# The recurrent block's six projected tiles as three quads of seven products

## The chip, the cores and the metric

The kernel runs on one core of one Trainium2 chip. The metric is device time in microseconds of one execution, as the median of several runs. Engines are TensorE (PE), VectorE (DVE), ScalarE (ACT), GpSimd (POOL) and SyncE (SP), which issues all DMAs. Each has a queue of its own and runs it in order; they are tied together by semaphores alone. All data is 32-bit float.

## What is computed

A stack of layers over 528 positions of width 1024. The change touches the first mixer, a gated recurrence of width 1536, cut here to what matters:

```python
def recurrent_mixer(x, w_in, conv_w, conv_b, w_r, b_r, w_i, b_i, lam, w_out):
    gr = x @ w_in
    gate, rec = gr[..., :D_RNN], gr[..., D_RNN:]
    rec = causal_dwconv(rec, conv_w, conv_b)          # width 4
    h = rg_lru(rec, w_r, b_r, w_i, b_i, lam)
    return (jax.nn.gelu(gate) * h) @ w_out

def rg_lru(x, w_r, b_r, w_i, b_i, lam):
    r = sigmoid(block_diagonal(x, w_r) + b_r)
    i = sigmoid(block_diagonal(x, w_i) + b_i)
    log_a = -LRU_C * r * softplus(-lam)
    a = exp(log_a)
    u = sqrt(-expm1(2.0 * log_a)) * (i * x)
    h_t = a_t * h_{t-1} + u_t                          # a scan over positions
```

## The kernel before

Features lie on the 128 partitions, positions along the row. The 1536 features of the recurrence are 12 tiles of 128, done in four groups of three. A group uses 8 weight units of 512 KB (`units`), which SP brings in order into the four slots of `W` (`w_ring`); the rule for when a slot may be overwritten is `slot_left`.

One group before, on PE (`with pe.Fori(0, 4)`): three dense tiles for the convolved half, a fourth for one gate, each a full product of 8 contraction steps by two halves of 264 positions, 16 matmuls (L2126, in `gemm`). Then the two block-diagonal products of the group (L2294, 28 matmuls), which wait for the three convolutions (`lru_conv`) and read them (`rc`). Then two more gate tiles. Tiles go through four PSUM buffers of two banks; `tile_full` and `tile_free` count them. ACT copies each tile from PSUM to `xp`, does the first convolution tap (L2471), the gelus, the sigmoids, exponentials and roots. DVE does the other three taps (`lru_conv`, L2729 and L2731), the squares (L2738, L2739), then for each tile two multiplies and the scan (L2743 to L2745) and the last multiply into `A` (L2748). POOL has nothing to do in this stage. When the last group is done, `lru_out` begins, the output projection.

`lru_out` and all feed-forward layers use another scheme, in `quads` (L2191). Two output tiles by two halves of the positions, with the contraction cut in two halves, are a 2 x 2 by 2 x 2 matrix product of blocks, and that is done with seven block products in place of eight. Four sums of weight blocks are made first by POOL (L2823, L2826, L2828, L2831, function `weights`), four sums of the moving blocks by DVE (`moving`, L2549 to L2557), and the results are put together from PSUM by copies on ACT (L2360) and sums on DVE (for instance L2675). Products are numbered 1 to 7 and run as 1, 2, 6, 7, 4, 5, 3; products 1, 6, 7, 4 add up in one bank, from which ACT copies a state after each of them ("kept" 1 to 4); the others are added to a kept state by DVE, giving results "11", "22" and "12", while kept 4 is "21". Two quads, each with 14 products together, run side by side, so that while PE does a product of one, the copies and sums of the other are made.

## Time and profile before

| | |
|---|---|
| median of 3 runs | 3436.01 us (3434.14 to 3436.01) |
| the profiled execution | 3435.82 us |
| its span | 3434.1 us |
| PE busy | 3265.1 us, 95% |
| DVE, POOL, ACT busy | 1686.8, 1121.7, 1031.5 us |
| recurrent stage | about 6 to 219 us |

The page lists busy time by engine, the chain of work that ended last and the costliest groups of instructions. The timeline gives each engine's instructions in order of time, merged where neighbours are alike, with the idle time before them and its releaser in brackets. A matmul of 32-bit data leaves two records, so "x32" is 16 matmuls, and a product of a quad with four contraction steps is eight records. PE records overlap: the start of the next group is the better end of a group than start plus length.

### The profile page before, as it was taken

What the parts mean: (1) busy time and instruction counts of PE and PEld (TensorE: products, weight loads), DVE (VectorE), ACT (ScalarE), POOL (GpSimd) and SP (SyncE); (2) the same over time, 40 slices, a digit from 0 to 9 for tenths busy, and PEclk for the clock granted to TensorE, in tenths of its full rate; (3) what the DMA queues carried; (4) which work ended last, traced back from release to release, by engine and by line L of the source; (5) the groups of instructions that cost most, each with busy time, mean ns of one, the idle gap of its engine ahead of it and who ended that gap; (6) DMA issues with size and microseconds to landing.
All of it is one profiled execution on the core that took longest, in us unless ns stands there. A gap on an engine that the chain in (4) does not pass through costs nothing.

```text
span 3434.1 us, 51574 instructions
## 1 busy us (share of the span) xinstructions
PE 3265.1 (95%) x16950; PEld 2639.6 (77%) x16950; DVE 1686.8 (49%) x2837; ACT 1031.5 (30%) x2083; POOL 1121.7 (33%) x908
## 2 busy tenths in 40 slices
PE   9999999989998999998999999989999899799997
PEld 7787888867776788886546787868888588688886
DVE  3454546464445445644446545354553534355544
ACT  3433232122332323212316333123321334222311
POOL 0023344432221335441001333434444232353543
PEclk9999999999999999998999999989999899999999
DMA  3222222211111222221210211212222121122222
GB/s 119 79 86 92 79 92 80 92 68 51 54 50 38 74 83 82 80 92 56 68 55 19 62 55 55 80 55 92 79 92 82 66 68 63 50 74 91 85 92 74
DMA packets 68670, 249.36 MB, mean 73 GB/s; under 512 B 7568, under 2 KB 7568, under 8 KB 68544
## 3 DMA queue, kind: packets, MB, share of 16 engines
q1 hardware_dynamic: 68544, 247.72, 21.1%
q8 instruction: 75, 1.23, 0.1%
q14 instruction: 51, 0.42, 0.0%
HBM read 245.59 MB, written 2.10 MB: 72 GB/s over the span
## 4 chain that ended last, share of the span: by engine, by line
PE 88%; DVE 7%; issue 2%; ACT 2%; DMA 0%; DVEq 0%; POOL 0%; ACTq 0%; SPq 0%; POOLq 0%
PE psum L2191 54%; PE psum L2126 10%; PE psum L434 6%; PE psum L1745 3%; PE psum L1303 3%; PE psum L1330 1%; PE psum L1770 1%; PE psum L2294 1%; PE psum L466 1%; PE psum L1357 1%; PE psum L504 1%; DVE residual L2652 1%; PE psum L2245 1%; DVE stream L2650 1%; ACT scratch L1036 1%
## 5 line engine op out<-in xcount | busy, mean ns | idle before, releaser
L2191 PE MATMUL psum<-scratch 128*128 128x256 f32 (+1 forms) x3600 | 816.7, 383 | 12.3 <-ACT scratch L2360 6.4
L2191 PEld LDWEIGHTS psum<-scratch 128*128 128x128 f32 x3600 | 684.4, 190 | 120.2 <-ACT scratch L2360 8.9
L2823 POOL TENSOR_TENSOR scratch<-w_ring 128x512 f32<-128x512 f32 (+2 forms) x160 | 201.7, 1261 | 1374.1 <-DMA w_ring<-units 807.2
L2360 ACT ACTIVATE scratch<-psum 128x264 f32<-128x264 f32 (+1 forms) x480 | 185.0, 387 | 890.2 <-PE psum L2191 855.2
L2675 DVE TENSOR_TENSOR scratch<-scratch,psum 128x264 f32<-128x264 f32 (+1 forms) x264 | 108.3, 424 | 503.2 <-PE psum L2191 475.2
L2191 PE MATMUL psum<-scratch,w_ring 128*128 128x256 f32 (+1 forms) x1200 | 275.6, 382 | 0.0
L2191 PEld LDWEIGHTS psum<-scratch,w_ring 128*128 128x128 f32 x1200 | 227.9, 190 | 34.9
L2191 PE MATMUL psum<-acts,w_ring 128*128 128x264 f32 (+1 forms) x1088 | 247.1, 385 | 2.6 <-ACT scratch L2475 1.1
L2191 PEld LDWEIGHTS psum<-acts,w_ring 128*128 128x128 f32 x1088 | 207.7, 191 | 35.6 <-issue 2.5
L2423 ACT ACTIVATE scratch<-scratch,params 128x528 f32<-128x528 f32 (+1 forms) x176 | 144.4, 821 | 274.8 <-DVE scratch L2675 274.8
L2828 POOL TENSOR_TENSOR scratch<-w_ring 128x512 f32<-128x512 f32 (+2 forms) x160 | 226.5, 1416 | 0.0
L2831 POOL TENSOR_TENSOR scratch<-w_ring,scratch 128x512 f32<-128x512 f32 (+2 forms) x160 | 223.6, 1398 | 2.6 <-PE psum L2191 2.6
L2826 POOL TENSOR_TENSOR scratch<-scratch,w_ring 128x512 f32<-128x512 f32 (+2 forms) x160 | 219.5, 1372 | 12.6
L2682 DVE SCALAR_TENSOR_TENSOR scratch<-scratch,params 128x528 f32<-128x528 f32 (+1 forms) x176 | 201.6, 1145 | 25.5 <-DVE scratch L2680 8.9
L2680 DVE SCALAR_TENSOR_TENSOR scratch<-scratch,params 128x528 f32<-128x528 f32 (+1 forms) x176 | 203.9, 1158 | 0.0
L2126 PE MATMUL psum<-residual,w_ring 128*128 128x264 f32 (+1 forms) x800 | 181.9, 390 | 6.3 <-DMA residual<-x_t 6.3
L2126 PE MATMUL psum<-stream,w_ring 128*128 128x512 f32 (+1 forms) x400 | 178.6, 602 | 1.0 <-DVE stream L2637 1.0
L2126 PEld LDWEIGHTS psum<-residual,w_ring 128*128 128x128 f32 (+1 forms) x800 | 149.7, 188 | 37.9 <-issue 8.0
L2191 PE MATMUL psum<-residual,w_ring 128*128 128x264 f32 x704 | 165.3, 394 | 3.5 <-ACT residual L2407 3.5
L2191 PE MATMUL psum<-stream,w_ring 128*128 128x256 f32 x704 | 159.8, 386 | 1.9 <-DVE stream L2637 1.9
L2191 PEld LDWEIGHTS psum<-residual,w_ring 128*128 128x128 f32 x704 | 137.0, 195 | 28.3 <-issue 4.0
L2191 PEld LDWEIGHTS psum<-stream,w_ring 128*128 128x128 f32 x704 | 136.6, 194 | 21.7 <-issue 2.5
(454 smaller groups left out, 4732.9 us busy)
## 6 DMA issues: line engine op xcount, KB each, us to landing
w_ring<-units SPq DMA_DIRECT2D x463, 512.0 KB, 3.6
residual<-x_t SPq DMA_DIRECT2D x4, 528.0 KB, 7.0
out_t<-residual SPq DMA_DIRECT2D x4, 512.0 KB, 2.7
params<-cols SPq DMA_DIRECT2D x1, 568.5 KB, 9.1
gate_w_sb<-gate_w SPq DMA_DIRECT2D x1, 96.0 KB, 11.2
```

Source lines behind the costliest of these rows:

```text
L434: mm = nc.tensor.matmul(fx_bank(p), weights(k), moving(k), start=(p in (1, 2, 5) and k == 0), stop=(k == 3), skip_group_check=True)
L2126: mm = nc.tensor.matmul(PS[0:m1 - m0, bank + b, 0:n], W[:, s, q, m0:m1], rhs(k)[:, t:t + n], start=(k == 0), stop=(k == slots[-1][1] + slo ...
L2191: mm = nc.tensor.matmul(out, weights(k), moving(k), start=(p in (1, 2, 5) and k == 0), stop=(k == h - 1), skip_group_check=(p != 2))
L2360: nc.scalar.activation(kept(q, n, H), quad_bank(q, p, H), ACT.Copy).then_inc(q_copied, 1)
L2423: nc.scalar.activation(y[:, j, 0:T], xp[:, j, 0:T], ACT.Identity, bias=w(3), scale=w(0)).then_inc(shared("tap", name), 1)
L2675: v.tensor_tensor(xp[:, row, at:at + H], kept(q, keep, H), quad_bank(q, p, H), ALU.add).then_inc(q_added, 1)
L2680: c(v.scalar_tensor_tensor(out=y[:, j, 0:T], in0=xp[:, j, 1:1 + T], scalar=PAR[:, ds(w0 + 1, 1)], in1=y[:, j, 0:T], op0=ALU.mult, op1=ALU. ...
L2682: v.scalar_tensor_tensor(out=y[:, j, 0:T], in0=xp[:, j, 2:2 + T], scalar=PAR[:, ds(w0 + 2, 1)], in1=y[:, j, 0:T], op0=ALU.mult, op1=ALU.ad ...
L2823: g.tensor_tensor(s(1), row(1, 0), row(1, 1), ALU.add).then_inc(q_weight, 1)
L2826: g.tensor_tensor(s(2), s(1), row(0, 0), ALU.subtract).then_inc(q_weight, 1)
L2828: g.tensor_tensor(s(3), row(0, 0), row(1, 0), ALU.subtract).then_inc(q_weight, 1)
L2831: g.tensor_tensor(s(4), row(0, 1), s(2), ALU.subtract).then_inc(q_weight, 1)
```

## The change

The six projected tiles of a group (three for the convolution, three for the gates) become three quads m = 0, 1, 2, each making two tiles: quad 0 makes convolved tiles 0 and 1, quad 1 convolved tile 2 and gate 0, quad 2 gates 1 and 2. Quads 0 and 1 run side by side; quad 2 follows with its products 1, 2 and 6, the first block set, product 7, the second block set, and products 5, 4, 3. Units of the two block sets stand at the end of a group's eight. The loop over groups is written out on every engine. POOL makes twelve weight sums a group, DVE nine result sums, ACT twelve copies; the gelu now reads SBUF. The four moving sums of the input are made once, at the start, into `Z`. The start of SP's list is changed: the parameters come after the first four units.

```diff
+LQ_PRODUCTS = [(p, m) for p in (1, 2, 6, 7, 4, 5, 3) for m in (0, 1)] + [(p, 2) for p in (1, 2, 6, 7, 5, 4, 3)]
+LQ_WEIGHTS = [(n, m) for ns in ((1, 2), (3,), (4,)) for m in (0, 1) for n in ns] + [(n, 2) for n in (1, 2, 3, 4)]
+LRU_BANK = (0, 2, 6)
...
+                if name == "lru" and u < end:
+                    i, j = divmod(u, 8)
+                    if j >= 6:
+                        return [(tile_full, 6 * i + 3 * (j - 5))]
+                    return [(q_product, lq_done(i, j // 2, 4 if j % 2 else 2)), (q_weight, lq_weighed(i, j // 2, 3 if j % 2 else 4))]
...
+            for b in (2, 1, 3):
+                sp.dma_start(W[:, b, :, :], units[b]).then_inc(w_full[b], 16)
             sp.dma_start(PAR[:, :], cols).then_inc(loaded, 16)
-            for b in range(1, SLOTS):
-                sp.dma_start(W[:, b, :, :], units[b]).then_inc(w_full[b], 16)
...
+            for i in range(GROUPS):
+                for p, m in LQ_PRODUCTS[:14]:
+                    lru_quad(i, m, p)
+                for p in (1, 2, 6):
+                    lru_quad(i, 2, p)
+                pe.wait_ge(S("lru_conv"), 3 * i + 3)
+                pe.wait_ge(q_copied, lq_kept(i, 1, 4))
+                pe.wait_ge(q_added, lq_added(i, 1, "12"))
+                lru_blocks(i, 0)
+                lru_quad(i, 2, 7)
+                lru_blocks(i, 1)
+                for p in (5, 4, 3):
+                    lru_quad(i, 2, p)
...
+            for i in range(GROUPS):
+                lru_sum(i, 0, "11")
+                lru_sum(i, 1, "11")
+                if i:
+                    lru_scan(i - 1)
+                lru_sum(i, 0, "22")
+                lru_sum(i, 1, "22")
+                lru_conv(i, 1)
+                lru_sum(i, 0, "12")
+                lru_sum(i, 1, "12")
+                lru_conv(i, 0)
+                lru_sum(i, 2, "11")
+                lru_conv(i, 2)
+                if i == GROUPS - 1:
+                    dve.wait_ge(S("lru_act"), 9 + 1)
+                    for n in range(1, 5):
+                        moving(CHUNKS["lru_out"], n, 4, acts_of(0), HALF, T1)
+                lru_sum(i, 2, "22")
+                lru_squares(i)
+                lru_sum(i, 2, "12")
+            lru_scan(GROUPS - 1)
...
+            for i in range(GROUPS):
+                for n, m in LQ_WEIGHTS:
+                    lru_weights(i, n, m)
+            pool.wait_ge(q_product, lq_done(GROUPS - 1, 2, 3))
             down("lru_out")
```

In `lru_quad`, product 6 waits for weight sum 2 and kept state 1, product 7 for weight sum 3 and kept 2, product 4 for kept 3, product 5 for weight sum 1 and result "11", product 3 for weight sum 4 and result "22". `lru_sum` waits for its product and kept state. ACT's list in a group is: kept 1 of quads 0 and 1, the last group's roots, kept 2, gelus of the last group between kept 3 of quads 0 and 1, kept 4 and the taps, kept 1 and 2 of quad 2, sigmoids around its kept 3, exponentials and tanhs with its kept 4.

PE, the end of a group's first part and the first block set. Before (the fourth dense tile, then the wait for `lru_conv`):

```order
L2114 REGISTER_ALU [waits w_full3]
L2126 MATMUL psum<-residual,w_ring 128x264 [waits tile_free]
L2126 MATMUL psum<-residual,w_ring 128x264 x15
L2286 ISA
L2109 REGISTER_ALU [waits lru_conv]
L2114 REGISTER_ALU [waits w_full0]
L2294 MATMUL psum<-scratch,w_ring 128x264 [waits tile_free]
```

And now, from product 3 of quad 1 to the second block set (L2356 is a product, L2368 the blocks):

```order
L2356 MATMUL psum<-residual,scratch 128x264 [waits quad_added,quad_weight]
L2356 MATMUL psum<-residual,scratch 128x264 x3
L2356 MATMUL psum<-residual,w_ring 128x264 [waits w_full0,quad_copied]
L2356 MATMUL psum<-residual,w_ring 128x264 x3
L2356 MATMUL psum<-residual,w_ring 128x264 [waits w_full0,quad_added]
...
L2356 MATMUL psum<-stream,scratch 128x264 [waits quad_copied,quad_moving,quad_weight]
...
L2368 MATMUL psum<-scratch,w_ring 128x264 [waits w_full2,quad_added,tile_free,quad_copied,lru_conv]
...
L2368 MATMUL psum<-scratch,w_ring 64x264 x4
L2368 MATMUL psum<-scratch,w_ring 32x264 x4
L2356 MATMUL psum<-stream,scratch 128x264 [waits quad_copied,quad_moving,quad_weight]
...
L2368 MATMUL psum<-scratch,w_ring 128x264 [waits tile_free,w_full3]
```

The dense tile of 16 matmuls ahead of the wait for `lru_conv` has become three products of four, and a fourth stands between the two block sets.

DVE, around the squares and the scan. Before, in one row after the convolutions (L2738 and L2739 squares, L2743 to L2745 multiplies and scan):

```order
L2738 TENSOR_TENSOR scratch<-scratch 128x528 [waits lru_at]
...
L2739 SCALAR_TENSOR_TENSOR scratch<-scratch 128x528 [waits dve_chain]
...
L2743 TENSOR_TENSOR scratch<-scratch 128x528 [waits lru_sqrt]
...
L2744 TENSOR_TENSOR scratch<-scratch 128x528 [waits dve_chain]
...
L2745 SCALAR_TENSOR_TENSOR scratch<-scratch 128x528 [waits dve_chain]
...
L2747 ISA [waits dve_chain]
L2748 ISA [waits tile_free]
```

And now, from the last sum of group 0 on (L2866 is a result sum, L2888 to L2890 the scan of the last group, L2893 the last multiply, L2872 a convolution step):

```order
L2866 TENSOR_TENSOR scratch<-scratch,psum 128x264 [waits quad_copied,quad_product]
L2866 TENSOR_TENSOR scratch<-scratch,psum 128x264 [waits lru_conv,quad_copied,quad_product] x2
L2888 TENSOR_TENSOR scratch<-scratch 128x528 [waits tile_free,lru_sqrt]
L2889 TENSOR_TENSOR scratch<-scratch 128x528 [waits dve_chain]
L2890 SCALAR_TENSOR_TENSOR scratch<-scratch 128x528 [waits dve_chain]
...
L2893 TENSOR_TENSOR acts<-scratch 128x528 [waits lru_gelu,dve_chain]
...
L2866 TENSOR_TENSOR scratch<-scratch,psum 128x264 [waits lru_conv,quad_copied,quad_product]
L2866 TENSOR_TENSOR scratch<-scratch,psum 128x264 [waits lru_conv,lru_act,quad_copied,quad_product]
L2872 SCALAR_TENSOR_TENSOR scratch<-scratch,params 128x528 [waits lru_tap]
```

The scan and the multiplies of a group have moved behind the first two result sums of the next, and stand ahead of the two that follow.

## Rows read from the trace of the kernel before

**Rows 1.** The page: busy time (1), chain by engine (4).
```profile
PE 3265.1 (95%) x16950; PEld 2639.6 (77%) x16950; DVE 1686.8 (49%) x2837; ACT 1031.5 (30%) x2083; POOL 1121.7 (33%) x908
...
PE 88%; DVE 7%; issue 2%; ACT 2%; DMA 0%; DVEq 0%; POOL 0%; ACTq 0%; SPq 0%; POOLq 0%
```

**Rows 2.** Timeline of PE: start, length, record count; idle before in brackets.
```profile
99.62 42.99 PE L2126 MATMUL psum<-residual,w_ring 128*128 128x264 f32 x192
142.45 9.87 PE L2294 MATMUL psum<-scratch,w_ring 128*128 128x264 f32 x56
152.24 42.99 PE L2126 MATMUL psum<-residual,w_ring 128*128 128x264 f32 x192
```

**Rows 3.** Waits of PE, 0 to 240 us: total, times, longest.
```profile
PE psum L2191 <- ACT scratch L2475: 1.1, 1, 1.1
```

**Rows 4.** Windows: busy us by engine, PEclk, DMA share, GB/s.
```profile
100.00:150.00 50.00, 50.00 (x232) 41.28 (x230) 21.13 (x27) 23.55 (x31) 0.00 (x0) 1.00 0.24 78
```

**Rows 5.** Timeline of PE in the quads of lru_out.
```profile
245.92 7.28 PE L2191 MATMUL psum<-acts,w_ring 128*128 128x264 f32 x32
253.04 7.28 PE L2191 MATMUL psum<-acts,scratch 128*128 128x264 f32 x32
```

**Rows 6.** Tile w_ring, 353.8 to 355 us: DMA issues, time to landing.
```profile
L2090 SPq DMA_DIRECT2D w_ring<-units x2: 328/355/382, 353.6 to 354.0; - x2
...
DMA to landing us min/median/max: 3.5/4.0/4.4
```

**Rows 7.** Timeline of DVE and ACT, 57 to 74 us, POOL idle.
```profile
59.79 0.71 DVE L2743 TENSOR_TENSOR scratch<-scratch 128x528 f32<-128x528 f32 x1
...
62.57 0.71 DVE L2743 TENSOR_TENSOR scratch<-scratch 128x528 f32<-128x528 f32 x1
...
65.56 1.95 DVE L2748 TENSOR_TENSOR acts<-scratch 128x528 f32 x3 [0.25 <-DVE scratch L2745]
...
69.69 0.83 ACT L2471 ACTIVATE scratch<-scratch,params 128x528 f32<-128x528 f32 x1 [0.18 <-ACT scratch L2468]
...
72.52 0.77 DVE L2731 SCALAR_TENSOR_TENSOR scratch<-scratch,params 128x528 f32<-128x528 f32 x1
```

**Rows 8.** Timeline of DVE and POOL, 215 to 241 us, both busy.
```profile
217.06 1.66 DVE L2744 TENSOR_TENSOR scratch<-scratch 128x528 f32<-128x528 f32 x1
...
218.75 2.21 DVE L2745 TENSOR_TENSOR_SCAN scratch<-scratch 128x528 f32<-128x528 f32 x1
...
226.55 4.98 DVE L2748 TENSOR_TENSOR acts<-scratch 128x528 f32<-128x528 f32 x3
...
240.64 1.27 POOL L2823 TENSOR_TENSOR scratch<-w_ring 128x512 f32<-128x512 f32 x1 [7.98 <-PE psum L2191]
```

**Rows 9.** Lines L2675 (a DVE sum reading PSUM) and L2360: ns min/median/max, mean.
```profile
L2675 DVE TENSOR_TENSOR scratch<-scratch,psum x264: 411/423/431, 320.0 to 3277.6; 128x264 f32<-128x264 f32 x66, 128x256 f32<-128x256 f32 x66
...
L2360 ACT ACTIVATE scratch<-psum 128x264 f32<-128x264 f32 (+1 forms) x480 | 185.0, 387 | 890.2 <-PE psum L2191 855.2
```

**Rows 10.** Waits of DVE, 0 to 240 us.
```profile
DVE small L2708 <- DMA params<-cols: 12.3, 1, 12.3
```

**Rows 11.** Tile w_ring, first units: issue times and landing.
```profile
L2085 SPq DMA_DIRECT2D w_ring<-units x3: 432/451/870, 3.7 to 4.7; - x3
...
DMA to landing us min/median/max: 9.8/11.0/11.8
```

**Rows 12.** Timeline of PE, first group.
```profile
8.38 28.99 PE L2126 MATMUL psum<-residual,w_ring 128*128 128x264 f32 x124 [0.33 <-DMA residual<-x_t]
```

**Rows 13.** Idle PE and its clock after: timeline of PE, windows.
```profile
792.35 0.45 PE L488 MATMUL psum<-identity,scratch 128*128 128x128 f32 x1 [2.82 <-DVE scratch L667]
...
2945.87 7.13 PE L2191 MATMUL psum<-scratch 128*128 128x256 f32 x24 [4.98 <-POOL scratch L2826]
...
792.00:794.00 2.00, 1.65 (x5) 1.32 (x6) 1.01 (x5) 1.97 (x3) 2.00 (x3) 0.59 0.00 0
2946.00:2948.00 2.00, 2.00 (x6) 1.58 (x7) 0.00 (x0) 0.00 (x0) 2.00 (x2) 0.54 0.18 72
```

More of the change, by code:

```diff
@@ new lines, in lru_blocks, with piece @@
+            def lru_blocks(i, g):
+                s = unit(0, i, 8, 6 + g)
+                at = 3 * g
+                def piece(o, k, b, t, n, first=False):
+                    (r0, r1), (c0, c1) = LRU_CROSSED.get((o, k), ((0, P), (0, P)))
+                    return nc.tensor.matmul(PS[c0:c1, LRU_BANK[o] + b, 0:n], W[r0:r1, s, LRU_PIECES.index((o, k)), c0:c1],
+                                            rc[r0:r1, k, t:t + n], start=first, stop=not first, skip_group_check=True)
+                for o in range(3):
+                    pe.wait_ge(tile_free, 6 * i + (at + o + 1 + BUFS - 3))
+                    for b, t, n in parts(T1):
+                        piece(o, o, b, t, n, True)
+                for pair in LRU_PAIRS:
+                    for b, t, n in parts(T1):
+                        for o, k in pair:
+                            mm = piece(o, k, b, t, n)
+                            if b == 1 and (o, k) == (0, 1):
+                                mm.then_inc(tile_full, 1)
+                            if b == 1 and (o, k) == (2, 1):
+                                mm.then_inc(tile_full, 2)
@@ L2371, in down @@
                 for c in range(len(KS[name])):
+                    if name == "lru_out" and c == 0:
+                        body(0, b, (2, 3))
+                        body(1, b)
+                        continue
                     if name == "mix_out" and c == 0:
@@ L2493, in _ @@
+            lru_roots(GROUPS - 1)
+            copies(0, BODIES["lru_out"], T1, (1,))
+            for j in range(3):
+                lru_gelu(GROUPS - 1, j)
             project("lru_out", T1)
@@ L2546, in moving @@
                 if n == 1:
+                    if chunk == CHUNKS["lru"]:
+                        for q in range(4):
+                            dve.wait_ge(x_loaded[q], 16)
                     if chunk >= 2:
@@ L2911, in _layout @@
             put(a_in, RNN + (3 * g + j) * P)
-        put(a_in, 3 * g * P)
+        for j in range(3):
+            put(a_in, (3 * g + j) * P)
         for w in (f["a_w_r"][0], f["a_w_i"][0]):
@@ L2919, in _layout @@
             at[0] += 1
-        for j in (1, 2):
-            put(a_in, (3 * g + j) * P)
     at_phase("lru_out")
```

284 lines of the change are left out of this document (183 added, 101 removed).

## The prediction

> **What bounds the kernel now.** The page first: TensorE (PE) is busy for 95% of the span, and the chain that ended last is PE's work for 88% [rows 1]. So a stage is worth what PE spends in it. The timeline of PE in the recurrent stage comes next [rows 2]: each trip is one unbroken run of 192 records at L2126 and one of 56 at L2294 (every matmul leaves two records, and a product of four matmuls eight). From 99.62 to 142.45 us is 42.83 us for the 192, to 152.24 another 9.79 us for the 56: 52.62 us a group, no gap. Once the first input is there, PE waits for another engine once up to 240 us, for 1.1 us [rows 3]. VectorE (DVE) works 21 us in each 50 of this stage and GpSimd (POOL) not at all [rows 4]. The stage is bound by PE alone; the others have slack that the change spends.
>
> **What it removes.** A quad does 7 products of 4 matmuls for the 32 matmuls of two projected tiles. A group falls from 96 matmuls to 84. The existing quads show the pace: 32 records, 4 products, from 245.92 to 253.04 us, 7.12 us, or 1.78 us a product [rows 5]. 21 products are 37.4 us; with the blocks' 9.79 us, 47.2 us a group. Against 52.62 that is 5.45 us a group, **21.8 us in four groups**. The wait of 1.1 us for a gelu at the head of the output projection [rows 3] goes as well. All the rest of the change is waits, so I walked through one group, queue by queue; numbers that follow another engine's step include its wake-up, 0.2 to 0.3 us. E is the end of the second block set; a product is 1.78.
>
> **Weights, each boundary between groups.** Unit 9 may be fetched only after product 4 of quad 2, at E+3.56, and unit 10 stands behind it on SP's queue. PE has the product 3 and the next product 1, 3.56 us, before it reads unit 10. A row shows such a pair: issued 353.56 and about 0.47 later, landing after 3.5 and 4.4 us [rows 6], so the second is there 4.9 us after the first was issued. With 0.2 us to wake SP and 0.1 to wake PE: 5.2 - 3.6 = **1.6 us**, four times (the head of lru_out has it too). Bounds: 0.9 (landings 0.6 shorter) to 2.0.
>
> **DVE's queue, the scan.** The scan of the last group now stands between two quad sums. It starts when sum "11" of quad 1 is done: E + 5.34 (products 5, 4, 3) + 1.6 + 4 products + 0.3 + 0.43 = E+14.8. Alone its nine instructions take 3 x 2.78 us (59.79 to 62.57), the three multiplies 2.1 with their wake [rows 7]: done at E+25.2, and sum "22" of quad 0, due at E+26.8, is on time. But POOL now forms twelve weight sums a group. What this does is in the rows where POOL and DVE first meet [rows 8]: DVE instructions with both inputs in SBUF go from 0.71 us (at 59.79, [rows 7]) to 1.66, 0.95 us more for each POOL instruction beside them, and the scan from 1.26 to 2.21; three multiplies take 4.98 instead of 1.95 us. The sums that read PSUM stay at 0.42 us [rows 9]. POOL's eight sums for quads 0 and 1 run from E+7.5 (landing of unit 9) to about E+20.7, the four for quad 2 from E+26.9. The scan meets three to four of the first, the multiplies two of the others: 5.2 us. DVE reaches sum "22" at E+30.4, and product 3 of quad 0 starts at E+31.0 in place of E+28.3: **2.7 us**. Bounds: 0 (without the meetings) and 4.
>
> **DVE's queue, the convolution.** Before, the blocks waited for three convolutions under the gate tile of 7.2 us; now the cover is products 1, 2, 6 of quad 2, 5.34 us, after product 3 of quad 1. In that time DVE finishes conv 1, does sums "12" of quads 0 and 1, conv 0, sum "11" of quad 2 and conv 2. A tap is 0.83 us and ends at 70.52, the third instruction of its convolution at 73.29: 2.6 us and 0.17 to wake [rows 7]. With a POOL instruction beside conv 1, conv 2 ends 8.4 us after that product 3, PE asks at 5.34 + 0.4 (product 6 waits for a copy behind the taps): **2.8 + 0.4 us**, each group. Without POOL it is 2.1.
>
> These rows have DVE lose 0.95 us beside a POOL instruction that alone takes 1.27 [rows 8]. The Trainium skill ("SBUF — State Buffer", Who interferes with whom) has the loser of the shared port blocked for the other's whole instruction. By that, six meetings a group cost 0.3 us more each; the sum goes by the rows, and the rest is rival E.
>
> **The start.** The parameters move behind three weight units on SP. They landed at 12.3 us, when their first user on DVE started [rows 10]; unit 2 takes that place and lands at about 12.1, while product 1 of quad 0 is done at 9.3: 2.8. Then units 1 and 3 at about 13.7 and 15.1 (the three landed 9.8 to 11.8 us after issues at 3.7 to 4.7, [rows 11]), each with two POOL sums before product 6: 0.7 and 1.1 more, and the blocks' 2.8: **7.5 us** in group 0, where before lost 1.2 (124 records from 8.38 us to the first block set at 37.20, 28.8 us where 27.7 would do [rows 12]).
>
> **Head of lru_out.** 1.6 for weights; POOL starts only after the last product and makes four sums for quad 0 before two for quad 1: 1.6; DVE brings the scan, four operand sums and a full backlog, so that product 3 waits 4.0. **7.2 us**, where before had 1.1 and about 0.5 [rows 3, 5].
>
> **Hidden.** ScalarE gets 12 copies of 0.387 us [rows 9] for three of 0.61, about 2.8 us a group, beside a similar set of table loads; it is ahead of PE at each copy by my walk except at the 0.4 above. Writing out the loop removes register work on queues that had slack. SP and DMA volume are unchanged.
>
> **The sum.** -21.8 + 7.5 + 3 x (1.6 + 2.7 + 0.4 + 2.8 = 7.5) + 7.2 - (1.2 + 1.1 + 0.5 saved) = **+12.6 us**. The profiled execution took 3435.8 (a span of 3434.1 and 1.7 around it), the median run 3436.0; forecast **3448.6 us**.
>
> **Rivals.** (B) *The clock follows the stalls.* After PE idled 4.98 us for a POOL sum, up to 2945.87 us, the granted clock was 0.54, where 0.50 is 1.2 GHz and 1.00 is 2.4, and 24 records took 7.13 us, where at the pace of [rows 5] 5.3 and a record's tail of 0.16 would do: 1.6 us lost. After a wait of 2.82 us, up to 792.35, it was 0.59 [rows 13]; there sparse small matmuls stood before it, here a dense stretch would. My stalls of 2.7, 2.8 and 4.0 us lie about there. 1.0 to 1.6 us for each of some seven such stalls, partly swallowed by the next wait: +4 to +10, 3456 us. The Trainium skill ("TensorE: Matmul & The Clock Gate", The HAM clock gate) has the array at 1.2 GHz when it has been idle and at 2.4 when busy, which speaks for B; these rows agree. (C) *DVE keeps up.* It decides at product 3 of quad 0: if the scan and multiplies meet POOL for 2.7 us less than I count, that stall is gone in three groups (-8.1), the convolutions' falls by 0.3 in four (-1.2) and that of lru_out by 2: 3437 us. For it speaks that POOL's start hangs on landings that spread by 0.9 us [rows 6], and that the overlap is worked out, not seen; against it, that every SBUF instruction of DVE beside POOL in [rows 8] pays. (D) *They do not meet at all*, POOL's sums falling into DVE's idle time: what stays is weights 4 x 1.6, convolutions 4 x 2.1 and 3.5 at the start, 18.3 us against the 24.6 saved: -6.3, 3429.5 us, on the other side. The place is the same queue; it decides where fewer than about one in five of the meetings happens. Against it: POOL needs 15 to 20 us of a group's 47 (twelve of 1.27 to 1.7) and DVE 27, in one order for both. (E) *A meeting costs the whole POOL instruction*, 1.27 us: 6 x 0.32 x 3 groups, +5.8, 3454 us; a backlog carried from group to group would end there or above, to 3460.
>
> **Chances.** Forecast 0.44, B 0.16, C 0.24, D 0.10, E 0.06. The forecast's own range, from the bounds on landings and on the scan's stall, is 3441 to 3453. The range of 3430 to 3459 leaves out half of D and the upper parts of B and E. 0.2% is 6.9 us, about what a measurement here can tell from no change: faster than 3429.1 has 0.09 (most of D's low half and of C's tail), slower than 3442.9 0.62 (B, E and the forecast less its low edge), the same 0.29.
>
> **What would show it.** Products 1.78 us apart and groups 54.7 us apart; PE waiting for a DVE sum before product 3 of quad 0, for a DVE convolution before each block set, and for a DMA of w_ring at the second product of each group; DVE's SBUF instructions at 1.7 us beside POOL. The profile that proves me wrong has groups under 50 us apart and PE without waits of over 1 us, or multiplies at 0.65 us right before the sums.

## The result, and the profile after

| | before | the change |
|---|---|---|
| median | 3434.14 us (3430.58 to 3436.01, 7 runs) | 3445.65 us (3444.51 to 3453.97, 7 runs) |
| profiled execution, its span | 3435.82, 3434.1 us | 3451.29, 3449.6 us |
| PE busy | 3265.1 us | 3257.4 us |

The ratio is 1.0037, with an interval of 1.0027 to 1.0048: slower by 0.37%. The forecast was 3448.6 us, 12.6 above before; the medians are 11.5 apart. The profiled execution of the change is 5.6 us slower than its median, so what its trace shows, the granted clock above all, is one case and not the average. On the page PE has less work, and its part of the chain has gone from 88% to 84%, where [rows 1] stood before:

```profile
PE 3257.4 (94%) x16854; PEld 2625.3 (76%) x16854; DVE 1735.6 (50%) x2877; ACT 1028.3 (30%) x2111; POOL 1196.6 (35%) x956
...
PE 84%; DVE 9%; issue 3%; ACT 3%; DMA 1%; POOL 0%; DVEq 0%; SPq 0%; ACTq 0%; POOLq 0%
```

What PE waited for between 0 and 290 us (total, times, longest), where [rows 3] had one wait of 1.1 us for another engine:

```profile
PE psum L2368 <- DVE scratch L2874: 7.7, 4, 1.9
PE psum L2356 <- DMA w_ring<-units: 6.0, 4, 1.7
PE psum L2356 <- DMA residual<-x_t: 5.8, 1, 5.8
PE psum L2230 <- DVE stream L2726: 4.6, 1, 4.6
PE psum L2230 <- POOL scratch L2982: 1.8, 1, 1.8
PE psum L2356 <- DVE scratch L2866: 1.6, 2, 0.8
PE psum L2230 <- DMA w_ring<-units: 1.5, 1, 1.5
```

L2356 is a product of the recurrent quads, L2368 a block set, L2230 a product of `lru_out`; L2874 ends a convolution, L2866 is a result sum. The third group in PE's timeline, where [rows 2] had one unbroken run:

```profile
107.57 2.05 PE L2356 MATMUL psum<-stream,scratch 128*128 128x264 f32 x8
109.46 1.94 PE L2356 MATMUL psum<-stream,w_ring 128*128 128x264 f32 x8
...
113.02 1.94 PE L2356 MATMUL psum<-residual,w_ring 128*128 128x264 f32 x8
116.33 5.58 PE L2356 MATMUL psum<-residual,w_ring 128*128 128x264 f32 x24 [1.37 <-DMA w_ring<-units]
...
144.22 2.02 PE L2356 MATMUL psum<-stream,scratch 128*128 128x264 f32 x8 [0.96 <-ACT scratch L2553]
148.18 6.67 PE L2368 MATMUL psum<-scratch,w_ring 128*128 128x264 f32 x28 [1.94 <-DVE scratch L2874]
154.78 2.05 PE L2356 MATMUL psum<-stream,scratch 128*128 128x264 f32 x8
156.66 4.88 PE L2368 MATMUL psum<-scratch,w_ring 128*128 128x264 f32 x28
161.47 2.05 PE L2356 MATMUL psum<-stream,scratch 128*128 128x264 f32 x8
```

Three things are to be read here. Products are 1.78 us apart where nothing waits, as forecast. The second block set ends at 107.57 and 161.47: this group lasted 53.90 us (the four ends are 55.33, 107.57, 161.47 and 215.46, so 52.24, 53.90 and 53.99). And a wait costs 0.16 us more than its bracket: from 113.02 to 116.33 are 3.31 us for one product and a wait of 1.37, since the last record's tail of 0.16 is in the open. The first block set of this group took 6.67 us where the second took 4.88. The windows say why (columns: stretch, sum, PE, PEld, DVE, ACT, POOL busy, PEclk, DMA share, GB/s):

```profile
95.00:98.00 3.00, 2.04 (x9) 1.78 (x10) 0.87 (x2) 0.00 (x0) 0.00 (x0) 1.00 0.03 14
148.20:153.20 5.00, 5.00 (x16) 3.68 (x18) 0.00 (x0) 0.00 (x0) 0.00 (x0) 0.66 0.00 0
202.30:207.30 5.00, 5.00 (x18) 3.40 (x20) 4.62 (x4) 0.00 (x0) 0.00 (x0) 0.66 0.01 3
```

After one and the same wait of 1.94 us the granted clock stayed 1.00 in the second group and was 0.66 over the block set in the third and the fourth. The head of `lru_out` has three waits, and the third leaves a clock of 0.66 (251 to 256 us) too, 5.51 us for 16 records that take 3.72 elsewhere:

```profile
224.39 5.58 PE L2230 MATMUL psum<-acts,w_ring 128*128 128x264 f32 x24 [1.54 <-DMA w_ring<-units]
...
233.59 5.60 PE L2230 MATMUL psum<-acts,scratch 128*128 128x264 f32 x24 [1.84 <-POOL scratch L2982]
...
250.87 5.51 PE L2230 MATMUL psum<-acts,scratch 128*128 128x264 f32 x16 [4.56 <-DVE stream L2726]
```

DVE and POOL in the second group, from the start of the scan (L2888 to L2890) over the three multiplies (L2893) to sum "22" (L2866) and the first convolution (L2872):

```profile
70.09 0.70 DVE L2888 TENSOR_TENSOR scratch<-scratch 128x528 f32<-128x528 f32 x1
70.83 1.66 DVE L2889 TENSOR_TENSOR scratch<-scratch 128x528 f32<-128x528 f32 x1
72.53 2.20 DVE L2890 TENSOR_TENSOR_SCAN scratch<-scratch 128x528 f32<-128x528 f32 x1
74.77 1.60 DVE L2888 TENSOR_TENSOR scratch<-scratch 128x528 f32<-128x528 f32 x1
...
81.21 3.04 DVE L2893 TENSOR_TENSOR acts<-scratch 128x528 f32<-128x528 f32 x3
84.17 0.76 DVE L2866 TENSOR_TENSOR scratch<-scratch,psum 128x264 f32<-128x264 f32 x2
...
82.42 1.27 POOL L3000 TENSOR_TENSOR scratch<-w_ring 128x512 f32<-128x512 f32 x1 [6.62 <-DMA w_ring<-units]
```

Three instructions of the scan pay for a POOL instruction beside them, 0.9 us each, as in [rows 8]. Of the multiplies only one does (3.04 us for three, about 1.1 above their time alone), since POOL's next sums start at 82.42, when two of them are through. In the third group none does, in the fourth one, and PE waits before product 3 of quad 0 in the second and the fourth group alone (0.78 and 0.77 us):

```profile
133.42 1.95 DVE L2893 TENSOR_TENSOR acts<-scratch 128x528 f32<-128x528 f32 x3
...
187.49 3.02 DVE L2893 TENSOR_TENSOR acts<-scratch 128x528 f32<-128x528 f32 x3
```

The scan here doesn't wait for the roots, which ACT ends at 69.60 us, but for its place behind sum "11" of quad 1 (69.75 us).

### The profile page after: what moved, and what is told of

Read it like the earlier page. It is cut to its first block, busy times and chain, and to the rows that moved or that the text cites. A ratio compares the mean times of both kernels' runs of the same rounds, so it can differ in the third digit from the quotient of the medians.

```text
span 3449.6 us, 51443 instructions
## 1 busy us (share of the span) xinstructions
PE 3257.4 (94%) x16854; PEld 2625.3 (76%) x16854; DVE 1735.6 (50%) x2877; ACT 1028.3 (30%) x2111; POOL 1196.6 (35%) x956
## 4 chain that ended last, share of the span: by engine, by line
PE 84%; DVE 9%; issue 3%; ACT 3%; DMA 1%; POOL 0%; DVEq 0%; SPq 0%; ACTq 0%; POOLq 0%
PE psum L2230 53%; PE psum L473 6%; PE psum L2165 5%; PE psum L1784 3%; PE psum L1342 3%; PE psum L2356 2%; PE psum L1369 1%; PE psum L2368 1%; PE psum L1809 1%; PE psum L505 1%; PE psum L1396 1%; DMA w_ring<-units 1%; PE psum L543 1%; DVE scratch L2872 1%; DVE residual L2784 1%
## 5 line engine op out<-in xcount | busy, mean ns | idle before, releaser
L2230 PE MATMUL psum<-scratch 128*128 128x256 f32 (+1 forms) x3600 | 816.7, 383 | 12.2 <-ACT scratch L2444 6.4
L2230 PEld LDWEIGHTS psum<-scratch 128*128 128x128 f32 x3600 | 684.4, 190 | 120.1 <-ACT scratch L2444 8.8
L2230 PE MATMUL psum<-scratch,w_ring 128*128 128x256 f32 (+1 forms) x1200 | 275.6, 382 | 0.0
L2230 PEld LDWEIGHTS psum<-scratch,w_ring 128*128 128x128 f32 x1200 | 227.9, 190 | 34.9
L2230 PE MATMUL psum<-acts,w_ring 128*128 128x264 f32 (+1 forms) x1088 | 248.0, 385 | 3.4 <-DMA w_ring<-units 1.9
L2230 PEld LDWEIGHTS psum<-acts,w_ring 128*128 128x128 f32 x1088 | 207.8, 192 | 36.9 <-issue 3.7
L2982 POOL TENSOR_TENSOR scratch<-scratch,w_ring 128x512 f32<-128x512 f32 (+2 forms) x160 | 220.1, 1376 | 12.6
L2230 PE MATMUL psum<-residual,w_ring 128*128 128x264 f32 x704 | 164.7, 393 | 3.5 <-ACT residual L2495 3.5
L2230 PE MATMUL psum<-stream,w_ring 128*128 128x256 f32 x704 | 160.0, 387 | 1.9 <-DVE stream L2769 1.9
L2230 PE MATMUL psum<-acts,scratch 128*128 128x264 f32 (+1 forms) x624 | 149.5, 392 | 10.1 <-DVE stream L2726 7.5
L2230 PEld LDWEIGHTS psum<-residual,w_ring 128*128 128x128 f32 x704 | 136.6, 194 | 28.0 <-issue 3.9
L2230 PEld LDWEIGHTS psum<-stream,w_ring 128*128 128x128 f32 x704 | 136.7, 195 | 21.8 <-issue 2.5
L2165 PEld LDWEIGHTS psum<-stream,w_ring 128*128 128x128 f32 (+1 forms) x400 | 75.1, 191 | 95.7 <-issue 93.8
```

What stands on the lines that cost most here:

```text
L2165: mm = nc.tensor.matmul(PS[0:m1 - m0, bank + b, 0:n], W[:, s, q, m0:m1], rhs(k)[:, t:t + n], start=(k == 0), stop=(k == slots[-1][1] + slo ...
L2230: mm = nc.tensor.matmul(out, weights(k), moving(k), start=(p in (1, 2, 5) and k == 0), stop=(k == h - 1), skip_group_check=(p != 2))
L2982: g.tensor_tensor(s(2), s(1), row(0, 0), ALU.subtract).then_inc(q_weight, 1)
```

## The experiments

Two theories came out of this reading. **The chain**: each wait is only where a chain shows that is as long as PE's own work in a group. It goes from the block sets over sigmoids, exponentials, squares, roots, scan and multiplies to sums "22", and PE's product 3 waits for them; taking one wait away then hands it on to the next. **The waits add up**: each is a local matter of its own, and goes with its own remedy. Beside them stands rival B, the clock. In every run, "distances" are those between the ends of the second block sets. "The first norm" is the start of the matmuls that follow `lru_out`, 296.82 us in before's profile and 308.17 in the change's; behind it the code of all kernels is the same.

**POOL's sums made thin.**

```diff
-                row = lambda r, half: W[:, slots[r], half * h:half * h + h, :]
-                s = lambda n: weight(m % 2, n)[:, :, :]
+                row = lambda r, half: W[:, slots[r], half * h:half * h + h, 0:8]
+                s = lambda n: weight(m % 2, n)[:, :, 0:8]
```

> The changed kernel, with POOL's twelve weight sums of a group in the recurrent block formed over 8 of 512 columns; the other columns of those sums are left at a constant, so this part is not computed. DVE then meets almost no POOL work until lru_out. Theory (contention in DVE's queue sets the scan stall and half of the convolution stall): the wait before product 3 of quad 0 (0.8 us in two of three groups) goes to 0, the convolutions of quad 0/1 run at 0.77 us a step, the wait before each first block set falls from 1.9 to about 1.3 us, the copies' wait before product 6 of quad 2 goes, groups are 51 us apart instead of 52.2 to 54. The wait for DVE at the head of lru_out falls from 4.6 by 1 to 2 us. In all 6 to 9 us faster than the changed kernel, about 3438 us. Rival (the stalls are the dependency chain of PE, ACT and DVE alone, contention costs nothing that PE sees): the same waits of 1.9 and 0.8 us stay, and the time with them, 3445 us.

3438.86 us; ratio to before 1.0007 (0.9998 to 1.0016). The wait before the block sets fell from 1.94 to 1.03 us in all four groups, that before product 3 went, the boundaries' waits for weights stayed, and so did DVE's 4.57 at the head of `lru_out`:

```profile
111.42 5.58 PE L2356 MATMUL psum<-residual,w_ring 128*128 128x264 f32 x24 [1.47 <-DMA w_ring<-units]
141.16 4.98 PE L2368 MATMUL psum<-scratch,w_ring 128*128 128x264 f32 x28 [1.03 <-DVE scratch L2874]
```

A group is 50.1 us, 3.8 less than the two long ones of the change, of which 0.9 is the convolution's wait, 1.0 the wait for a sum or a copy (0.78 to 0.96 with its tail), and 1.7 the clock, which never fell in the groups (at the head of `lru_out` 16 records took 5.93 us behind the wait of 4.57). By the medians POOL's full sums cost 6.8 of the 11.5 us lost. By the traces it is more: at the first norm this profile stands at 295.81 us, 12.4 ahead of the change's and 1.0 ahead of before's, and what it lost after that arose in code that is the same. The run prices POOL's work as a whole, its meetings with DVE and PE's two waits for POOL at the start (0.36 and 0.60 us in the change) together; no run here takes them apart.

**The order of the weight units.** SP fetches units 8, 10, 11, 9 in place of 8, 9, 10, 11 in each later group, so that unit 10 no longer stands behind unit 9.

```diff
-            for n in range(SLOTS, N_UNITS):
+            fetch = list(range(SLOTS, N_UNITS))
+            for g in (8, 16, 24, 32):
+                fetch[g - SLOTS:g] = [g, g + 2, g + 3, g + 1]
+            for n in fetch:
```

> The changed kernel with one edit: at each boundary SP fetches units in the order 8, 10, 11, 9 in place of 8, 9, 10, 11, so that only the unit that waits for product 4 of quad 2 comes last. Theory: PE's waits for w_ring at the second product of groups 1 to 3 and of lru_out (1.4 to 1.5 us, 6.0 in all) vanish. DVE's scan starts that much earlier against POOL, so the wait before product 3 of quad 0 grows by up to 0.7 us in each group. Net -4 to -6 us: about 3441 us. Rival (the waits are only handed on: the DVE queue is the bound of a group, so PE waits the same time later in the group): group distance stays 52.2 to 54 us and the time stays 3445 us.

3447.3 us; 1.0031 (1.002 to 1.0042): nothing gained. The waits at the boundaries are gone, and product 3 of quad 0 waits in their place. From PE's timeline:

```profile
86.08 3.80 PE L2359 MATMUL psum<-residual,scratch 128*128 128x264 f32 x16 [2.55 <-DVE scratch L2869]
...
140.26 5.31 PE L2359 MATMUL psum<-residual,scratch 128*128 128x264 f32 x16 [4.38 <-DVE scratch L2869]
...
193.71 5.49 PE L2359 MATMUL psum<-residual,scratch 128*128 128x264 f32 x16 [3.19 <-DVE scratch L2869]
```

Distances are 52.4, 54.6 and 53.6 us, in sum within 0.5 us of the change's. The term "weights" of 1.6 us was right in size and worth nothing to remove: DVE's sum comes when the chain lets it, and PE is only there sooner.

**More cover for the convolutions.** Product 7 of quad 2 goes ahead of the first block set, product 5 between the two.

```diff
-                for p in (1, 2, 6):
+                for p in (1, 2, 6, 7):
...
-                lru_quad(i, 2, 7)
+                lru_quad(i, 2, 5)
...
-                for p in (5, 4, 3):
+                for p in (4, 3):
```

> The changed kernel with product 7 of quad 2 moved ahead of the first block set and product 5 between the two block sets, so the convolutions have 7.12 us of cover instead of 5.34. Theory: the wait for DVE before the first block set, 1.94 us in each of four groups, falls to 0.2 to 0.4; and the slow runs of that block set (6.67 and 6.62 in place of 4.98 us, at a granted clock of 0.63 to 0.74) disappear because no wait of 1.9 us stands before it: -6.4 us of waits, -3.4 us of clock in a run like the profiled one; about 3437 us. Rival (clock falls have to do with the blocks' sparse shape or come by chance, not with the wait): waits fall, but two of four block sets still take 6.6 us; 3440 us. Second rival: product 7 waits for the copy behind the taps, and the time is unchanged.

3448.79 us; 1.0038 (1.0025 to 1.0051), where 3437 was expected. It goes as in the last run: the wait of 1.94 us is gone (0.57 for a copy stands there), product 3 waits 2.68, 2.92 and 2.95 us, and its 16 records take 5.34 to 5.48 us at the lower clock.

**The head of the output projection.** The moving sums of the second part are made behind the first body of `lru_out` in place of ahead of it.

```diff
+                    if name == "lru_out" and part == 0:
+                        body(0)
+                        dve.wait_ge(S("lru_act"), 12 + 1)
+                        for n in range(1, 5):
+                            moving(chunk + 1, n, 2, acts_of(1), H, T)
+                        body(1)
+                        continue
...
-            dve.wait_ge(S("lru_act"), 12 + 1)
-            for n in range(1, 5):
-                moving(CHUNKS["lru_out"] + 1, n, 2, acts_of(1), T1 // 2, T1)
```

> The changed kernel with the four moving sums of the second part of lru_out made after the first body's result sums, not before them. Theory: DVE reaches the sums that product 3 waits for at least 4 us earlier, so the wait of 4.6 us at 246 to 251 us falls below 0.5, and the 1.8 us that the next sixteen records lost to a lower clock go too: -5 to -6 us, about 3440 us. Rival (the wait is made by the scan of the last group itself, and the movings would be contended wherever they stand): -1 us at most and a new wait before product 6 of the second part.

3443.4 us; 1.002 (1.0011 to 1.0029): 2.3 us below the change by the medians, 5.0 at the first norm. This wait belonged to no chain: 4.56 us became 0.18, and the 16 records behind it took 3.83 us. The four groups are as before, with block sets of 4.99, 4.98, 6.67 and 6.62 us. In this profile the first group took back 3.0 us (24 records in 8.60 us after a wait of 1.76, where the change took 5.58 after 1.67).

**The scan earlier.** Its first tile goes ahead of sums "11", and ACT makes the roots ahead of its copy of product 1 of quad 1.

```diff
+                if i:
+                    lru_scan(i - 1, (0,), ())
                 lru_sum(i, 0, "11")
                 lru_sum(i, 1, "11")
                 if i:
-                    lru_scan(i - 1)
+                    lru_scan(i - 1, (1, 2))
```

> The changed kernel with the scan of the last group's first tile placed ahead of sums "11" of quads 0 and 1 on DVE, and the roots on ScalarE ahead of its copy of kept 1 of quad 1, so that the scan starts when its inputs are there and not when PE's second product of quad 1 is. Theory (DVE's queue is held up by the order in which it stands, not by its amount of work: it idles 13.7 us under the block sets): the scan starts about 3 us earlier, the waits before product 3 of quad 0 (0.8 us twice) go, the rest stays: convolution waits of 1.9, w_ring waits of 1.5; groups 52.2 us apart, -1.6 us, 3444 us, and slack of about 2 us in DVE's queue that the other edits can use. Rival (the queue is full: all that POOL shifts comes back): the same 0.8 us waits stay.

3444.46 us; 1.002 (1.0011 to 1.003). PE no longer waits before product 3, but the four waits before the block sets are 1.93 to 1.94 us as ever. Only the second of them was followed by a slow block set (6.62 us; the others 4.98).

**All four at once.**

> The changed kernel with four edits together: fetch order 8, 10, 11, 9 (as in e2_fetch), product 7 ahead of the first block set (as in e3_cover), the second part's moving sums after the first body (as in e4_head) and the earlier scan (as in e5_early). Theory (the edits of e2 and e3 were handed on to the scan's wait because DVE was late there by up to 3 us; with the scan 3 us earlier they count): groups 48.5 to 50 us apart, a head of lru_out with under 3 us of waits, 256.2 us of the changed kernel's start of the second body down to 238 to 242, and 3427 to 3433 us, below the kernel before. Rival (DVE together with POOL is the bound of a group at about 52 us): group distance stays at 51 to 53 us, time 3440 us.

3447.03 us; 1.0032 (1.002 to 1.0043). Expected were 3427 to 3433. Each edit that had removed its wait by itself was in, and PE waited before product 3, longer from group to group (distances 51.8, 54.4 and 55.1 us):

```profile
86.03 3.80 PE L2359 MATMUL psum<-residual,scratch 128*128 128x264 f32 x16 [2.65 <-DVE scratch L2876]
...
138.91 5.49 PE L2359 MATMUL psum<-residual,scratch 128*128 128x264 f32 x16 [3.73 <-DVE scratch L2876]
...
194.27 5.18 PE L2359 MATMUL psum<-residual,scratch 128*128 128x264 f32 x16 [4.66 <-DVE scratch L2876]
```

From the end of the second block set to sum "22" this profile has 29.1 us (109.25 to 138.35), some 9 of them what DVE lost beside POOL; PE has about 25 us of products in that time (14 of 1.78). From the first square at 114.08 us to sum "22" DVE is never idle: the chain is, in its greater part, DVE's own queue. The waits don't add up; the chain sets the group.

**The same with POOL's first sums for quad 1 ahead of those for quad 0.**

```diff
-LQ_WEIGHTS = [(n, m) for ns in ((1, 2), (3,), (4,)) for m in (0, 1) for n in ns] + [(n, 2) for n in (1, 2, 3, 4)]
+LQ_WEIGHTS = [(1, 1), (2, 1), (1, 0), (2, 0)] + [(n, m) for n in (3, 4) for m in (0, 1)] + [(n, 2) for n in (1, 2, 3, 4)]
```

> As e6_combo, and POOL forms sums 1 and 2 of quad 1 before those of quad 0, since with this fetch order the units of quad 1 land 3.6 us earlier. Theory: POOL ends its eight sums 3 us earlier, the scan meets fewer of them and the squares one or two more; -0.5 us a group against e6_combo. Rival: the squares, now under POOL, delay the roots and the scan by the same amount: equal to e6_combo or 0.5 us a group slower.

3446.35 us; 1.0028 (1.0016 to 1.004). The waits moved to ACT's copies (2.95, 1.26 and 2.48 us, one in each later group) and to POOL at the start (3.33 us); one of 2.66 us before product 3 stayed. The time can't tell the two expectations apart; the distances (53.6, 54.3 and 51.8 us) are 0.5 us a group shorter than the last run's.

**One wait made longer.** The change, with two more sums of 528 columns on DVE in the third convolution.

```diff
+                for _ in range(2 if j == 2 else 0):
+                    c(v.tensor_tensor(NORM_R[:, :], rc[:, 0, :], rc[:, 1, :], ALU.add))
```

> The changed kernel with two additional DVE sums of 128x528 chained into the third convolution of each group, so that the wait before the first block set grows from 1.9 to about 3.4 us. Theory B (the granted clock falls after waits of PE of about this length): the block set after it runs at a lower clock in at least three of four groups, 6.6 us or more in place of 4.98, where the changed kernel had it in two of four; so +6 us for the waits and +3 to +5 us for the clock, 3455 us. Rival (the falls have nothing to do with the length of the wait): 6.6 us in two of four or fewer, +6 us only, 3452 us.

3459.35 us; 1.0066 (1.0052 to 1.0081), 13.7 us above the change. The waits before the block sets are 3.42 us, 1.48 longer, 5.9 us in all; most of the rest is the clock: all four first block sets are slow now, 6.67, 6.67, 6.39 and 7.75 us, together 4.2 us more than the change's four, and 24 records at the start, behind a wait of 1.78 us for weights, took 8.58 us (5.58 in the change). That slow stretch is not of the edit's making, since it lies ahead of the first convolution; it would make up 3.0 of the 4.4 us by which 3455 was missed. Windows over the second and the fourth block set, PEclk third from the end:

```profile
103.20:108.20 5.00, 4.98 (x16) 3.70 (x18) 0.00 (x0) 0.00 (x0) 0.00 (x0) 0.66 0.00 0
...
213.80:218.80 5.00, 4.97 (x11) 3.87 (x12) 4.74 (x4) 0.00 (x0) 0.00 (x0) 0.50 0.02 3
```

**The multiplies taken out of the chain.** What has to be done before the sums "22" is the scan, whose inputs in `rc` the next taps overwrite, and, before that of quad 1, the first multiply, which reads the gate tile that this sum overwrites. In the change, one multiply goes between the two sums "22" and two behind the convolutions, with sum "11" of quad 2 behind them; the waits of ACT and DVE for the multiplies are moved to fit.

```diff
-                    lru_scan(i - 1)
+                    lru_scan(i - 1, (0, 1, 2), ())
                 lru_sum(i, 0, "22")
+                if i:
+                    lru_scan(i - 1, (), (0,))
                 lru_sum(i, 1, "22")
...
                 lru_conv(i, 0)
+                lru_conv(i, 2)
+                if i:
+                    lru_scan(i - 1, (), (1, 2))
                 lru_sum(i, 2, "11")
-                lru_conv(i, 2)
```

> In each of the four groups the multiply of state and kept factor is split: its first product is computed between the two sums "22" of the group's last product, the other two behind the convolution of the next group, so that the last sums of a group no longer stand behind three multiplies on VectorE (3.04 us for three in the profile of the change, 1.0 each). Chain theory: the distance between block sets of two groups is set by the chain from the block sets through sigmoids, roots, scan and multiplies to the last sums. Then 2 us of 53.9 leave each group: distances 51.5 to 52.5, the wait before the block sets (1.94 us) falls below 1, and the time is 3435 to 3441 us against 3445.7 for the change. Rival, several waits of nearly one size: the convolution comes later behind one multiply less only if the scan is not late; the wait turns up before the quad products for copies of ScalarE or for weights, distances stay 53 to 54 and the time is 3443 to 3449.

3442.67 us; 1.0023 (1.0014 to 1.0032). Between the theories: distances of 55.2, 52.3 and 51.7 us, waits before the block sets of 1.60 us (not below 1), all four block sets at full clock (4.98). The first distance holds a wait for weights of 3.34 us and a slow stretch behind it; the weight units fetched there took 6.4 us from issue to landing (median), where the change's took 4.0, and no edit here touches that. The expected time was missed by 1.7 us. The run decides little: at the first norm its profile is 1.6 us behind the change's (309.81 us).

**All remedies and the split.** Also ACT's copies of product 1 of `lru_out` ahead of the last group's roots, products 1 and 2 of quad 0 ahead of those of quad 1 (in every group), and the last group's multiplies behind the first body of `lru_out`.

> The change with all orders that the last runs point to at once: weight units in the order 8, 10, 11, 9; product 7 ahead of the first block set; the second part's moving sums behind the first body; the scan's first tile ahead of the sums "11"; multiplies split as in the run above; ScalarE's copies of product 1 ahead of the roots. Chain theory: the first combination (3447.0) kept the chain of about 29 us from block sets to last sums because it left the three multiplies (4.08 us with GpSimd beside them) in it; taking two of them out and starting the scan earlier leaves about 25 us against some 26 us of products, so groups of 49 to 50.5 us, and 3427 to 3434 us. Rival, a second chain as long: ScalarE's copies and GpSimd's sums hold the buffers of the quads, groups stay 52 to 54 us apart and the time is 3443 to 3449 us.

3430.06 us (3423.89 to 3436.42, 12 runs); before, in the same session, 3436.06. Ratio 0.9985 (0.9977 to 0.9994): faster than both kernels. Distances 49.5, 49.8 and 49.5 us. Waits of PE, 0 to 290 us, and its timeline over one group:

```profile
PE psum L2359 <- DMA residual<-x_t: 6.0, 1, 6.0
PE psum L2359 <- ACT scratch L2556: 4.4, 8, 0.8
PE psum L2359 <- POOL scratch L3018: 4.0, 5, 1.9
PE psum L2233 <- POOL scratch L2997: 2.8, 1, 2.8
```

```profile
105.92 2.05 PE L2359 MATMUL psum<-stream,w_ring 128*128 128x264 f32 x8
...
119.13 5.61 PE L2359 MATMUL psum<-stream,scratch 128*128 128x264 f32 x24 [0.48 <-POOL scratch L3018]
...
139.75 2.02 PE L2359 MATMUL psum<-stream,scratch 128*128 128x264 f32 x8 [0.76 <-ACT scratch L2556]
142.34 2.02 PE L2359 MATMUL psum<-stream,scratch 128*128 128x264 f32 x8 [0.57 <-ACT scratch L2556]
144.19 4.88 PE L2371 MATMUL psum<-scratch,w_ring 128*128 128x264 f32 x28
...
155.69 2.05 PE L2359 MATMUL psum<-stream,w_ring 128*128 128x264 f32 x8
```

No wait in a group is over 0.8 us, and the clock over the block sets is 1.00. Sum "22" comes 25.1 us after the block sets (81.50 us in the second group), with DVE again without idle time from the squares on.

**The same without product 7 ahead of the first block set.**

> As the run above without product 7 ahead of the first block set. The cover lengthens the stretch before the sigmoids of the second quad can start and shortens the one behind it. Chain theory: without cover the convolution's wait of 1.9 us comes back in each group (4 times, 7.7 us) but the scan is early by one product of 1.8 us; the time is 3431 to 3440 us. Rival: both waits stand (before block sets and before product 3), 3443 to 3449 us.

3430.81 us; 0.9989 (0.998 to 0.9998). Distances 50.1, 50.1 and 50.3 us. The convolution's wait came back (1.58 to 1.60 us, four times), the waits for copies and POOL became smaller, and the clock held. The cover is worth about half a microsecond a group (1.35 us at the first norm).

**The multiplies put back**, and nothing else, in the fast combination.

```diff
-                    lru_scan(i - 1, (1, 2), ())
+                    lru_scan(i - 1, (1, 2), (0, 1, 2))
                 lru_sum(i, 0, "22")
-                if i:
-                    lru_scan(i - 1, (), (0,))
...
-                if i:
-                    lru_scan(i - 1, (), (1, 2))
```

> The fast combination (3430.1 us, groups 49.5 to 49.8 us apart) with one thing undone: the three multiplies stand again in one piece between the last tile of the scan and the sums "22", in each of the three inner groups. Chain theory: they are a link of the chain from the block sets to the last sums, so all but what the chain had in hand comes back: the two multiplies that move stand 1.3 to 3.3 us in the way (0.7 us each alone, 1.66 beside GpSimd), three times, which makes groups of 51 to 52.5 us and 3434 to 3440 us. Rival: it was the other three edits between the combinations (ScalarE's copies of product 1 ahead of the roots, the products' order at the start, the last group's multiplies behind the first body) that made the difference; then the distances stay at 49.5 to 50.3 and the time is within 3429 to 3432 us.

3448.54 us; 1.0035 (1.0021 to 1.0048): by the medians 18.5 us above the fast combination, of which 13.0 are there at the first norm, from the place of three multiplies. Distances 56.5, 51.8 and 54.4 us. DVE's multiplies in the three groups, POOL beside the first, then PE's product 3 in that group:

```profile
80.83 5.06 DVE L2905 TENSOR_TENSOR acts<-scratch 128x528 f32<-128x528 f32 x3
...
137.34 3.01 DVE L2905 TENSOR_TENSOR acts<-scratch 128x528 f32<-128x528 f32 x3
...
189.16 4.08 DVE L2905 TENSOR_TENSOR acts<-scratch 128x528 f32<-128x528 f32 x3
...
80.69 1.26 POOL L3011 TENSOR_TENSOR scratch<-w_ring 128x512 f32<-128x512 f32 x1 [4.54 <-DMA w_ring<-units]
...
86.38 6.60 PE L2359 MATMUL psum<-residual,scratch 128*128 128x264 f32 x16 [4.70 <-DVE scratch L2878]
```

In this group POOL starts its sums for quad 2 just as the multiplies start, so all three pay: 5.06 us. Sum "22" runs at 85.81 us, 30.1 after the block sets, where the fast combination has 25.1. PE waits 4.70 us and then runs 16 records in 6.60 in place of 3.72 us: 7.7 us for a chain that had become 5.0 longer. Over the three groups the wait follows the multiplies: 4.70, 2.66 and 3.74 us for multiplies of 5.06, 3.01 and 4.08. The chain theory is right in kind. Its time of 3434 to 3440, 4 to 10 us above the fast combination, was too low: of the 13.0 at the first norm some 4.5 are the clock, which it left out, and the rest lies within it. The rival is out: the other three edits are all still in. At the first norm this profile is at 304.80 us against 291.77, at the end 20.0 behind; the other 7.0 arose in code that is the same.

## Why the prediction was right, and where only the sum was

Its points were that the products save 5.45 us a group, that PE, which waited for nothing, would wait for weights, for DVE's sums and for the convolutions, and that this costs more than is saved. All three hold. The terms, measured between points of PE's timeline up to the first norm (296.82 us before, 308.17 after):

| term | forecast | profile |
|---|---|---|
| start, against before's own loss | +6.3 | +4.8 |
| three groups, 52.62 before | +6.2 | +2.3, of it 3.3 clock |
| saving of the last group | -5.45 | -5.4 |
| head of `lru_out` | +5.6 | +8.6, of it 1.7 clock |
| from there to the first norm | 0 | +1.1 |
| sum | +12.6 | +11.4 |

The first is 55.33 - 46.99 less the two products that now stand earlier; the groups are 215.46 - 55.33 against 3 x 52.62; the head is 220.90 to 256.22 against 26.7 us before, its wait included.

- **The saving** was right: 1.78 us a product, and 5.4 us in the last group, where no wait lies between the points.
- **Weights, each boundary**: 1.6 forecast, 1.37 to 1.54 and the tail of 0.16 measured. Right in size; but the step "the sum" treated it as a loss of its own, and the run with another fetch order showed that it was slack that the chain had to spare.
- **The scan**: the step that failed. Forecast 2.7 us, measured 0.78, 0 and 0.77 with a tail of 0.16 to each wait. The start was right to the tenth (70.09 is E+14.8), and the scan met POOL three times. But the multiplies met it once, not at all and once, not twice in each group, since they started before POOL's next sums; so in the second group sum "22" came at E+28.8, not E+30.4. The run with the multiplies put back shows the other side of that narrow pass: there they start 0.14 us behind POOL's sum, here 1.21 ahead of it, and there all three meet. That no group of the change met more than one was decided by about a microsecond, which the prediction had no way to tell.
- **The convolution**: 2.8 + 0.4 forecast, 1.94 and the tail measured. The step "without POOL it is 2.1" was mis-sized: with thin POOL sums it is 1.03. POOL's part was 0.9 us for 0.7 forecast. The 0.4 for a copy was 0.27, 0, 0.96 and 0 in the four groups.
- **The start**: 7.5 forecast; the weights were there 1.1 us sooner, POOL's sums cost 0.36 and 0.60 instead of 0.7 and 1.1.
- **The head of lru_out**: 1.54, 1.84 and 4.56 us for 1.6, 1.6 and 4.0, with a tail each 1.2 more than forecast in sum, and the clock's 1.7 besides.
- **Rival B**, at 0.16, took place in part, beside the forecast and not in its place: three of the waits were followed by a granted clock of 0.66, for 1.6 to 1.7 us each, 5.0 us. Its reason stands (the run with the longer wait had it in all four groups); its count of seven did not.
- **Rival C** had the right cause, fewer meetings. Without the clock the outcome would have lain between it (+1) and the forecast (+12.6): +11.4 less 5.0 is +6.4 us at the first norm.
- **Rival D** fell: in each group the scan met POOL three times.
- **Rival E** fell: a sum that takes POOL 1.26 to 1.27 us alone cost DVE 0.89 to 0.95, in the change as in [rows 8]. Both pay: POOL's sums took 1.5 to 1.7 us beside DVE. By the Trainium skill ("SBUF — State Buffer", SBUF: two separate sides) the one that starts second is blocked until the other's whole instruction is over; the trace does not show a price that high.

So the time was met with waits forecast about 6 us too long and no clock loss in the sum, which had 5.0; that the two errors nearly cancel is luck. Behind the first norm, where the work is the same, this profile lost another 4.1 us (3141.4 against 3137.3 us). The other profiles have 3131.6 to 3142.3 for the same stretch, and one kernel's runs spread by 12 us; what decides that was not found.

The gain of the fast combination over before is 5.05 us at the first norm (291.77), of 21.8 that the products save. Of the 16.8 that are missing, the start takes 4.1, the three groups 7.3 (49.6 us each for 47.2 of work) and the head of `lru_out` 4.6; waits for POOL of 1.95, 0.61 and 2.76 us are a large part of start and head.

## What to carry to other kernels

When an engine that never waited gets less to do, look for the longest chain of dependences through the other engines in one period, and compare its length with what is left of the first engine's work: where they are near each other, single waits only hand themselves on, and what helps is to take out of the chain each instruction that nothing in it needs. A wait is to be costed with the clock behind it, and an overlap of two engines that is decided by a microsecond is to be costed at both ends.

## What the runs showed of the hardware

- The clock after a wait inside dense work. Waits of 1.03 us (six) and 1.58 to 1.60 us (eight) ahead of a block set left it at full clock. After 1.93 to 1.94 us, 5 of 14 block sets in the change and three of the experiments were slow (6.62 to 6.67 us for 4.98); the change had two after the same wait as the two that were not. Of the stretches of this stage behind waits of 2.55 to 2.68 us for DVE, 2 of 5 were slow, of those behind 2.92 us and more all. At the start, where eight records stand between PE's first idle time and the wait for weights, it came sooner: waits of 1.25 to 1.67 us (four) left the 24 records behind them at 5.58 us, five of six of 1.76 to 2.25 us did not (7.26 to 8.60). The Trainium skill ("TensorE: Matmul & The Clock Gate", The HAM clock gate) has the array at the lower clock when idle; these rows show that after one and the same wait of about 2 us, or of 2.6, it can be at either level.
- The price of such a fall was 1.7 us where the granted clock over the stretch was 0.66, and 2.8 us where a first block set took 7.75 us for 4.98 (0.50).
- DVE's sums that read PSUM stayed at 0.42 to 0.43 us in the change with its 48 weight sums on POOL (36 of them, 0.415 to 0.430); DVE's instructions that paid had all their operands in SBUF.
